# Decay sums of a bidirectional scan: both directions on halves of the array's rows, with a predicated copy

## The reference, cut to what matters

```
def segsum(a):
    cum = jnp.cumsum(a, axis=-1)
    diff = cum[..., :, None] - cum[..., None, :]
    return jnp.where(tril, diff, -jnp.inf)
...
lmat = jnp.exp(segsum(a))
y_diag = jnp.einsum("bclgn,bcsgn,bgecls,bcsgep->bclgep", Cc, Bc, lmat, X)   # with X = x * dt
...
y = y_f + y_b + X * d_skip          # forward, backward (flipped), skip
```

## Time and profile before

| what | us |
|---|---|
| median of 3 runs | 1745.7 |
| lowest, highest | 1745.17, 1748.32 |
| span of the profiled execution | 1742.8 |
| scan stage, layer 0 (197 to 304 us of the span) | 107 |
| scan stage, layer 1 (1062 to 1168 us) | 106 |
| experts, layer 0 (from about 432 to 872) | 440 |

### The profile page before, as it was taken

The page is one execution under the profiler, slowest core; times in us unless marked ns, Lnnn a source line. Parts: engine busy times, 40 slices in busy tenths (PEclk is TensorE's granted clock), DMA queues, the critical chain, the costliest instruction groups (busy, mean ns, idle before and its releaser), DMA issues.

```text
span 1742.8 us, 23270 instructions
## 1 busy us (share of the span) xinstructions
PE 1694.6 (97%) x8975; PEld 1056.7 (61%) x8975; DVE 713.3 (41%) x1345; ACT 685.1 (39%) x1549; POOL 668.0 (38%) x536
## 2 busy tenths in 40 slices
PE   8999999999999999899999999999999999999997
PEld 6889877787434444343378898777864344443343
DVE  5728788524212212121276387865241212222122
ACT  5565787754211111111156567877541111111111
POOL 7888876894000000000077887768930000000000
PEclk9999999999999999999999999999999999999999
DMA  7554312667999999999954442227589999999997
GB/s 271 195 193 152 140 49 108 274 259 308 363 415 427 428 427 428 427 428 428 411 229 165 179 189 97 97 80 300 219 333 398 420 427 427 428 427 428 428 425 303
DMA packets 50707, 528.47 MB, mean 303 GB/s; under 512 B 5496, under 2 KB 8312, under 8 KB 20128
## 3 DMA queue, kind: packets, MB, share of 16 engines
q1 hardware_dynamic: 50560, 526.89, 74.2%
q0 software_dynamic: 32, 0.02, 0.0%
HBM read 525.82 MB, written 1.06 MB: 302 GB/s over the span
## 4 chain that ended last, share of the span: by engine, by line
PE 68%; DMA 9%; DVE 9%; SPq 5%; ACT 5%; issue 2%; POOL 1%; DVEq 0%; ACTq 0%
PE PS L1297 19%; PE PS L1325 10%; DMA view<-in_w_exp_down_dram 9%; PE PS L875 8%; PE PS L877 8%; PE PS L876 8%; SPq L678 5%; DVE view L2003 5%; PE PS L1237 2%; PE PS L1223 1%; DVE view L1999 1%; PE PS L1082 1%; PE PS L1224 1%; PE PS L863 1%; ACT view L1571 1%
## 5 line engine op out<-in xcount | busy, mean ns | idle before, releaser
L2370 POOL TENSOR_TENSOR view<-view,view 128x512 fp32r<-128x512 f32 x448 | 579.8, 1315 | 548.1 <-ACT view L1457 537.3
L1297 PE MATMUL PS<-view,view 128*64 128x512 f32 x2044 | 457.8, 600 | 15.1 <-issue 14.5
L1457 ACT ACTIVATE view<-view 128x512 fp32r<-128x512 f32 x448 | 275.1, 633 | 149.1 <-PE PS L877 146.9
L1297 PEld LDWEIGHTS PS<-view,view 128*64 128x64 f32 x2044 | 150.9, 138 | 292.0 <-issue 288.7
L875 PE MATMUL PS<-view,view 128*128 128x512 f32 x704 | 286.0, 406 | 5.6 <-POOL view L2370 3.7
L877 PE MATMUL PS<-view,view 128*128 128x512 f32 x704 | 275.5, 391 | 0.0
L876 PE MATMUL PS<-view,view 128*128 128x512 f32 x704 | 275.4, 391 | 0.0
L1325 PE MATMUL PS<-view,stb 128*64 128x512 f32 x1024 | 230.4, 597 | 8.4 <-DMA view<-in_w_exp_down_dram 5.5
L2270 DVE SCALAR_TENSOR_TENSOR view<-PS,gcol,view 128x512 fp32r<-128x512 f32 x64 | 48.1, 751 | 448.7 <-ACT view L1770 448.6
L875 PEld LDWEIGHTS PS<-view,view 128*128 128x128 f32 x704 | 132.8, 189 | 33.5 <-issue 5.8
L1325 PEld LDWEIGHTS PS<-view,stb 128*64 128x64 f32 x1024 | 71.3, 136 | 132.6 <-issue 117.0
(11 more groups left out here) (260 smaller groups left out, 2024.0 us busy)
## 6 DMA issues: line engine op xcount, KB each, us to landing
view<-in_w_exp_up_dram SPq DMA_DIRECT2D x56, 2048.0 KB, 25.8
view<-in_w_exp_down_dram SPq DMA_DIRECT2D x56, 2048.0 KB, 28.1
view<-in_w_mix_dram SPq DMA_DIRECT2D x54, 2048.0 KB, 7.7
view<-in_w_exp_gate_dram SPq DMA_DIRECT2D x52, 2048.0 KB, 28.8
view<-in_w_exp_gate_dram SPq DMA_DIRECT2D x20, 512.0 KB, 31.2
view<-in_w_exp_down_dram SPq DMA_DIRECT2D x20, 512.0 KB, 14.9
view<-in_w_exp_gate_dram SPq DMA_DIRECT2D x8, 1024.0 KB, 8.1
view<-in_w_exp_up_dram SPq DMA_DIRECT2D x8, 1024.0 KB, 9.3
```

The lines of the kernel that those rows point to most:

```text
L1297: ins = pe.matmul(bank(ph, name, j)[e * CAP:(e + 1) * CAP, :], xgT1[:, k, at + e * CAP:at + (e + 1) * CAP], rows, start=(k == 0), stop=(k ...
L1457: nc.scalar.activation(highs(chunk), weights(slot8, chunk), ACT.Copy).then_inc(*high_ready.up(ph))
L2370: g_.tensor_tensor(weights(low8, chunk), weights(slot8, chunk), highs(chunk), ALU.subtract).then_inc(*low_ready.up(ph))
```

## The change

Decay sums: the two directions are laid on rows 0 to 63 and 64 to 127. A product now contracts 64 rows: 32 rows hold the parts of a group's eight heads for one direction (three parts and a row group of zeros), and 32 hold a staircase that gives the mask. What selects the head and the mask is a constant, `turns`, made on the host and loaded once by a DMA from POOL's queue. So four products of 64 rows a direction take the place of one of 128 rows and 512 columns and four of 96 rows, and the two directions are issued in turns:

```diff
-                    for d in range(2):
-                        b = PS[:, 4 + d, :]
-                        pe.matmul(b, identb[:, :], maskb[:, d:d + 1, :].to_broadcast([P, 4, P]),
-                                  start=True, stop=False, skip_group_check=True)
-                        for n in range(4):
-                            hc = g * GH + q * 4 + n
-                            ins = pe.matmul(b[:, n * P:(n + 1) * P],
-                                            pick[:, hc:hc + 1].to_broadcast([3 * SSM_HEADS, P]),
-                                            cumT[:, c, d, :], start=False, stop=(n == 3),
-                                            skip_group_check=True)
+                    for n in range(4):
+                        for d in range(2):
+                            rows = slice(64 * d, 64 * d + 64)
+                            ins = pe.matmul(PS[:, 5 - d, n * P:(n + 1) * P], turns[rows, 4 * q + n, :],
+                                            cums[g // 2][rows, 2 * (g % 2) + c, :], start=True, stop=True)
```

The rows of sums are made in two halves (banks 6 and 7), each with a staircase product of 512 columns for each direction; ACT drains both:

```diff
-                        for c in range(TT):
-                            for d in range(2):
-                                n = (2 * c + d) * P
-                                ins = pe.matmul(PS[0:3 * SSM_HEADS, 6, n:n + P],
-                                                parts[:, c, d].rearrange("p s h -> p (s h)"), identb[:, :],
-                                                start=True, stop=True)
-                        ins.then_inc(*fill(ph, "cum"))
+                        for half in range(2):
+                            pe.wait_ge(*free(ph, "cum", half))
+                            for d in range(2):
+                                pe.matmul(PS[64 * d + 32:64 * d + 64, 6 + half, :], stairs[:, :],
+                                          identb[:, :].unsqueeze(1).to_broadcast([P, 4, P]), start=True, stop=True)
+                                for n in range(4):
+                                    x_ = (n % 2) * 2 * SSM_GROUPS + d * SSM_GROUPS + 2 * half + n // 2
+                                    ins = pe.matmul(PS[64 * d:64 * d + 32, 6 + half, n * P:(n + 1) * P],
+                                                    parts[:, x_].rearrange("p s h -> p (s h)"), identb[:, :],
+                                                    start=True, stop=True)
+                            ins.then_inc(*fill(ph, "cum", half))
```

DVE no longer adds the directions. It copies the forward one over the backward one where a 0/1 mask (`tris`, the strict triangle) says so, and the diagonal is then there once:

```diff
-                        v.tensor_tensor(Lm, PS[:, 5, :], Lm, ALU.add).then_inc(*drain(ph, "D", j, q))
+                        v.copy_predicated(Lm.rearrange("p (h l) -> p h l", h=4),
+                                          tris[:, :].bitcast(mybir.dt.uint16).unsqueeze(1).to_broadcast([P, 4, P]),
+                                          PS[:, 5, :].rearrange("p (h l) -> p h l", h=4)
+                                          ).then_inc(*drain(ph, "D", j, q))
```

The diagonal's other share goes into the factor that multiplied the tokens (`d_skip` before). DVE works it out once per chunk, at the end of steps 0 and 3, and POOL's `skipped(j)` waits for it; `skipped(0)` moves behind the casts' remainders of step 0:

```diff
+                def own_token(c):
+                    link(v.tensor_tensor(by_group, cbt[:, c * SSM_GROUPS:(c + 1) * SSM_GROUPS, :],
+                                         ident[:, :].unsqueeze(1).to_broadcast([P, SSM_GROUPS, P]), ALU.mult))
+                    link(v.tensor_reduce(cb_own, by_group, AX, ALU.add))
+                    co = coef[:, c, 0:SSM_HEADS]
+                    link(v.tensor_tensor(co.rearrange("p (g h) -> p g h", g=SSM_GROUPS), ...
+                    v.tensor_tensor(co, co, bc_d, ALU.add).then_inc(*scales_ready.up(ph))
...
                 to_end(0)
-                skipped(0)
                 for j in range(UNITS_SCAN):
...
                     fed(2 * j)
+                    if j == 0:
+                        skipped(0)
```

More of the change, by code:

```diff
@@ L110, in bucket_onehot, with head_turns @@
     return oh
+def head_turns():
+    a = np.zeros((P, (GH + 1) * P - 96), np.uint16)
+    one, least = 0x3F80, 0xF180
+    s = np.arange(P) // 4
+    for p in range(P):
+        d, r = divmod(p, 64)
+        for h in range(GH):
+            if r < 32:
+                a[p, h * P:(h + 1) * P] = one * (r % GH == h)
+            else:
+                a[p, h * P:(h + 1) * P] = one * ((r - 32 > s) if d else (r - 32 < s))
+        a[p, GH * P + p // 4] = least
+    return a
 def parts_of(n):
@@ L139, in mixer_fills @@
         if b == 7:
-            f += [(("cum",), 6)]
+            f += [(("cum", half), 6 + half) for half in range(2)]
     for c in range(CT + 3):
@@ L522, in encoder @@
         s_const = once("s_const")
-        s_constv = once("s_constv")
+        s_turns = once("s_turns")
         s_pool = once("s_pool")
@@ L996, in layer @@
                     pe.wait_ge(*out_of(ph, "p", 5, t))
-                pe.wait_ge(*out_of(ph, "cum"))
+                for half in range(2):
+                    pe.wait_ge(*out_of(ph, "cum", half))
                 def decay_sums(i):
@@ L1411, in unit @@
                     for t in range(TT):
[L1412 removed]
+                        ins = pe.matmul(PS[:, 7, TT * P:TT * P + 1], Sg[:, t, j * P:(j + 1) * P], one[:, :],
                                         start=(t == 0), stop=(t == TT - 1))
@@ L1553, in layer @@
                     if b == 7:
-                        act.wait_ge(*full(ph, "cum"))
-                        nc.scalar.activation(cumT.rearrange("p c d l -> p (c d l)"), PS[0:3 * SSM_HEADS, 6, :],
-                                             ACT.Copy).then_inc(*drain(ph, "cum"))
+                        for half in range(2):
+                            act.wait_ge(*full(ph, "cum", half))
+                            nc.scalar.activation(cums[half].rearrange("p n l -> p (n l)"), bank(ph, "cum", half),
+                                                 ACT.Copy).then_inc(*drain(ph, "cum", half))
                 for c in range(CT + 3):
@@ L1807, in _ @@
                     dve.sem_inc(over_drained[i][b].sem, 1)
-            v.memset(ones[:, :], 1.0).then_inc(s_constv, 1)
-            v.memset(onesb[:, :], 1.0).then_inc(s_constv, 1)
+            v.memset(one[:, :], 1.0).then_inc(s_const, 1)
+            v.memset(oneb[:, :], 1.0).then_inc(s_const, 1)
             for i in range(DEPTH):
@@ L2344, in _ @@
                                  pattern=[[sg, P]], channel_multiplier=-sg).then_inc(s_pool, 1)
-                g_.affine_select(out=maskb[:, d, :], in_=maskb[:, d, :], compare_op=ALU.is_ge, fill=-BIG, base=0,
-                                 pattern=[[sg, P]], channel_multiplier=-sg).then_inc(s_pool, 1)
-            const(g_.memset(pick[:, :], 0.0))
-            for n in range(3):
-                ins = g_.affine_select(out=pick[:, :], in_=pick[:, :], compare_op=ALU.not_equal, fill=1.0,
-                                       base=-n * SSM_HEADS, pattern=[[-1, SSM_HEADS]], channel_multiplier=1)
-                if n < 2:
-                    const(ins)
-            ins.then_inc(s_pool, 1)
             g_.affine_select(out=tris[:, :], in_=tris[:, :], compare_op=ALU.is_gt, fill=0.0, base=0,
```

99 lines of the change are left out of this document (57 added, 42 removed).

## The result

The changed kernel takes 1748.6 us (median of 11 runs, 1746.6 to 1750.9), the kernel before 1745.3 in the same comparison: a ratio of 1.0017, with a 95% interval of 1.0009 to 1.0025. So it is slower by 3 us (1.6 to 4.4), and not faster by 11. That is a change too small for the prediction's own line for slower (1749.2), but it lies outside its range of 1727 to 1744.

A forecast was written before the change was run, and what follows sets the result against it. PE was taken to bound the scan, with DVE close behind. The scan's 6.5 us a layer less 1.0 for the rows of sums gave 11.0 in all: 1731.8 from the profiled 1742.8, predicted as 1735, range 1727 to 1744.

The forecast's parts named there:

- What bounds the kernel: Scan: PE sets the pace, DVE is next with 10.8 of 87 us left; the scan's gain reaches the end one to one.
- PE, each step: Decay sums on PE: 0.98 us becomes 0.32 or 0.54; 0.60 saved a step, 19.2 over both layers.
- the overlapping end: Decay sums on PE if the two row halves overlap: four times 0.055, plus 0.10, so 0.32 us a step.
- Rival 5: Halves issued one after the other, each load waiting for the array; nothing saved, 1746 to 1748 us; chance 0.06.
- Rows of sums: PE's products for the rows of sums: 1.0 us more a layer, 2.0 in all (0.4 to 3.2).
- The copy: DVE, each step: the predicated copy replacing the sum takes 0.68 us, the same; at the dear end 1.20.
- Rival 4: Slower: the predicated copy costs 1.2 us, so DVE's time eats all that PE saves; 1753 us; chance 0.09.
- own_token: DVE, twice a layer: product, reduction, two small operations; 1.75 to 3.0 us a call, the second, behind step 3, costing all.
- POOL: its "Nothing": POOL: moving `skipped(0)` ahead of the first sum and the changed setup cost no time.
- The sum, DVE's limit: Scan's 14 steps: DVE needs 81 of 87 us with waits, so 6.0 is gained, not PE's 8.4.
- rival 1: DVE's limit as summed holds the gain: 1731 to 1739 us; chance 0.50.
- Rival 3: Handshakes eat half, or rows of sums cost their full 1.6, or experts start no earlier: 1741 to 1745 us; chance 0.18.

The follow-up runs named there:

- The edit to rho: Changed kernel with the product for rho on one SBUF input and two scalars instead of two SBUF inputs: 1738.5 us against 1745.7, ratio 0.9962.
- The run with both hindrances away: Changed kernel without own_token and with the product for rho on one SBUF input: 1726.4 us against 1745.6 for the kernel before, ratio 0.9888.

## Why the prediction was wrong, point by point

**What bounds the kernel: right for the old kernel, and passed on as forecast.** PE led, DVE was next, and what the scan loses comes out at the end: 772.5 against 773.0 us between the scans, and tails of equal length (582.4 both).

**PE, each step: right, and better than taken.** The eight sums take 0.23 us (0.22 in the working) and the way into them 0.10 (the 0.10 added for the first load), so the 0.32 of the overlapping end was right. The scores gave 0.05 more, and 0.70 is saved, not 0.60. Rival 5 is dead. The run with both hindrances away shows 4.8 us in eight steps.

**Rows of sums: right, but too dear.** Behind block 7 of layer 0, first row and the next product (seven rows between them):

```profile
110.72 0.39 PE L989 MATMUL PS<-identb,turns 128*32 128x512 bf16 x1
...
111.29 0.50 PE L897 MATMUL PS<-view,view 128*128 128x512 f32 x1
```

0.57 us against the 0.20 of the earlier trace rows, and the product ahead takes 0.32 (from 110.40) where 0.22 is usual: 0.5 more a layer, not 1.0. One after the other they would have taken 1.76, so the 32-column parts run beside each other. The drain on a change of tiling mode, for which the prediction named the Trainium skill (TensorEngine Tiling (Array Packing), Key Properties), is inside this 0.5 together with the staircases; no run shows it by itself.

**The copy: right.** 0.74, a little over 0.68, hidden. Rival 4 is dead.

**own_token: wrong, the first failed step.** It had 1.75 to 3.0 us a call, the first call in DVE's slack. Measured are 3.08 and 3.86 on DVE and 2.3 net a call in both places, 4.5 a layer on the mean in place of some 2 (my estimate of what the forecast's sum charged, the second call in full and the first almost free). Two things went wrong in the working. Only the large product was allowed to meet POOL, and the two small operations were priced at 0.2 by their size and by L2019, a row with one input; with two inputs, L2046 took 1.19 us both times, while its like, L2043, took 0.19 in the second call. As I read it, a small operation waits for what is left of POOL's instruction, whose remainders are 1.2 to 1.3 us long; the ends at 207.29 and 208.48 fit that to 0.1 us. The edit to rho tested the reading, and moving these two operations to POOL gave 6.5 us, about the 6.1 that DVE spent on them in both layers. And a wait of 0.49 us on DVE was taken for slack for the whole call, though PE's next work hung on the mix that stands behind it.

**POOL: its "Nothing" was wrong, too, by less.** The moved `skipped(0)` was asked only whether it makes POOL late. Without `own_token` it stands beside DVE's product of step 1, which took 1.50 us in place of 0.68.

**The sum, DVE's limit: wrong, the second failed step.** "DVE needs 76.2 + 1.75 to 3.0" and 2 to 3 us of waits, 81 of 87, was to leave a gain of 6.0 in the stretch. The mechanism was the right one (rival 1 was "DVE's limit"), but its size was read from an average. Without `own_token` the whole layer gave 2.1. The average of 76.2 us holds steps in which DVE waited for PE and met POOL less, beside packed ones at 5.94 us each; four of the 15 intervals of the kernel before (steps 4, 5, 12, 13) already ran at that pace, and the average over all 15 is 6.17. With 5.94 for all of them the stage would have been 89.1 us, 3.5 less than 92.6 in place of the 6.5, and that before 4.6 for `own_token`.

**The rivals.** The price of a slowdown was given to the copy. The operation that did it had been priced with its upper end in the sum, but no rival let it cost more than that. Rival 3 (handshakes, 1741 to 1745) comes nearest to what the cheap sums did alone: 0.998 without `own_token`, 1742 on the scale of the forecast.

In a sum, from the traces: the cheap sums gave 2 x 2.1, `own_token` took 2 x 4.5, and from one scan to the other 0.4 went to the rows of layer 1: 5.2 us lost. The stretch ahead of the first maximum was 1.8 us shorter in this profile, by chance as it seems, which leaves the 3.4 between the spans. The eleven executions say 3.0 (1.6 to 4.4), so 5.2 may be too much; the difference is open.

**What was to show it wrong.** "A copy at 1.0 or more, PE without holes, or an expert stage that grows": none of these came. PE had its holes, DVE was busy for 91% of the middle and not 95. The list had nothing on `own_token`'s length, which is what decided.

## What to carry to other kernels

Before a gain on the leading engine is summed, look for the steps in which the second engine already runs without a wait, and take its pace from those; an average over steps in which it waits is too low, and its busy time can hold waits for another engine's reads. Price a small operation with two SBUF inputs on DVE beside a busy POOL by the length of POOL's instruction (here up to 1.2 us in place of 0.2), not by its own size; giving it one input and two scalars, or moving it to POOL, was worth 6 to 10 us here. An edit that is worth little before a change (1.1 us a layer) can be worth five times that after it (5.1), so a change that moves the bound should be tried together with the relief of the next engine.

## What the runs showed of the hardware

Three things were not expected. The product for rho, one element in a partition, takes 0.22 us with two SBUF inputs or, beside POOL, up to 1.08, and 0.27 each time with one. Eight products of 64 rows and 128 columns on the two halves of the rows start within 0.23 us, so a pair costs about what one product did. And PE's granted clock fell behind some of the new waits. The 6 us behind PE's wait of 2.11 us, changed kernel:

```profile
210.00:216.00 6.00, 5.97 (x37) 4.89 (x37) 5.89 (x9) 4.20 (x14) 4.21 (x4) 0.72 0.00 0
```

0.72 of the full 2.4 GHz, so part of the stretch was at 1.2; ahead of it PE had stood for 1.10 and 2.11 us. In the run without `own_token` the 1.10 is there and the 2.11 is not, and the clock was 1.00 from 209 to 215. The fall cost little here: DVE is busy for 5.89 of the 6 us, and the interval from step 1 to step 2 is 5.67 us, DVE's packed pace. It went with 1.9 us more in layer 0 of the kernel before with `own_token` added, where PE leads, and in the changed kernel with the addition a deeper fall (0.50 for 6 us) went with 2.0. What a lower clock costs depends on who leads at that moment, and on how deep it falls. The clock is not a fixed answer to a wait, either: behind the same 2.11 us it was 0.72 in one layer of that kernel and 1.00 in the other.
